# SiLU of two layers' gates: from one ScalarE instruction to a tanh in two halves with the products on GpSimd and VectorE

## The reference

```python
# layer 2
o = jnp.concatenate([oa.reshape(B, S, -1), ob.reshape(B, S, -1)], -1) * jax.nn.silu(gate)
return o @ w_out
...
# layer 3
od = rmsnorm(od, g_sub_d) * (1.0 - lam_init)
o = jnp.concatenate([oc.reshape(B, S, -1), od.reshape(B, S, -1)], -1) * jax.nn.silu(gate)
return o @ w_out
```

## Time and profile before

| | |
|---|---|
| median of 3 runs | 906.92 us (903.67 to 908.23) |
| the profiled execution | 905.25 us, of which its span is 903.4 us |
| busy in the span | TensorE 97%, VectorE 73%, ScalarE 53%, GpSimd 9% |
| instructions | 13206 |

### The profile page before, as it was taken

How to read it: one execution, slowest core, us unless ns; L and a number is a source line. 1 busy time by engine, 2 the same in 40 slices (tenths; PEclk the granted TensorE clock), 3 DMA queues, 4 the chain that set the end, 5 groups by cost and what they waited for, 6 DMA issues and landing times.

```text
span 903.4 us, 13206 instructions
## 1 busy us (share of the span) xinstructions
PE 876.2 (97%) x4896; PEld 719.4 (80%) x4896; DVE 659.9 (73%) x1147; ACT 482.0 (53%) x872; POOL 77.5 (9%) x88
## 2 busy tenths in 40 slices
PE   8999999999999999999999999999889989999998
PEld 7777678888888887777888888888669858878876
DVE  6788876777774468877667777546588767999974
ACT  6367845444454355566544444436456675654771
POOL 2100000000000000000000000001385000122010
PEclk9999999999999999999999999999999999999999
DMA  9673146666666575533666666555954414654311
GB/s 344 225 225 117 45 137 195 186 187 186 188 187 187 159 225 171 158 103 113 204 193 186 187 186 186 186 186 151 237 177 142 133 39 132 198 164 127 87 44 46
DMA packets 96495, 147.58 MB, mean 163 GB/s; under 512 B 6240, under 2 KB 59648, under 8 KB 96304
## 3 DMA queue, kind: packets, MB, share of 16 engines
q1 hardware_dynamic: 94656, 141.63, 50.7%
q0 software_dynamic: 912, 2.41, 1.3%
q10 hardware_dynamic: 864, 2.70, 0.9%
HBM read 145.67 MB, written 1.05 MB: 162 GB/s over the span
## 4 chain that ended last, share of the span: by engine, by line
PE 82%; issue 6%; DVE 5%; DMA 3%; ACT 2%; POOL 1%; SPq 0%; DVEq 0%; ACTq 0%; POOLq 0%
PE ps L2319 17%; PE ps L2203 15%; PE ps L2205 14%; PE ps L2204 14%; PE ps L2321 8%; DMA w_raw<-in_w_in_e 3%; PE ps L2405 3%; PE ps L2382 3%; PE ps L2420 3%; POOL small L777 1%; PE ps L2174 1%; PE ps L2190 1%; DVE w_lo L1352 1%; PE ps L2280 1%; PE ps L2282 1%
## 5 line engine op out<-in xcount | busy, mean ns | idle before, releaser
L1352 DVE TENSOR_TENSOR w_lo<-w_raw,w_hi 128x1024 fp32r<-128x1024 f32 (+1 forms) x261 | 308.4, 1206 | 79.6 <-ACT w_hi L876 77.7
L876 ACT ACTIVATE w_hi<-w_raw 128x1024 fp32r<-128x1024 f32 (+1 forms) x261 | 263.6, 1036 | 111.8 <-DMA w_raw<-in_w_down 44.4
L2319 PE MATMUL ps<-hT,w_hi 128*128 128x512 f32 x640 | 226.5, 399 | 0.0
L2203 PE MATMUL ps<-w_hi,hT 128*128 128x512 f32 (+3 forms) x448 | 174.8, 390 | 7.4 <-ACT z L934 3.8
L2321 PE MATMUL ps<-hT,w_lo 128*128 128x256 f32 x640 | 179.8, 281 | 0.0
L2205 PE MATMUL ps<-w_lo,hT 128*128 128x512 f32 (+3 forms) x448 | 169.6, 379 | 0.0
L2204 PE MATMUL ps<-w_hi,hT 128*128 128x512 f32 (+3 forms) x448 | 169.5, 378 | 0.0
L2319 PEld LDWEIGHTS ps<-hT,w_hi 128*128 128x128 f32 x640 | 120.3, 188 | 29.9
L2321 PEld LDWEIGHTS ps<-hT,w_lo 128*128 128x128 f32 x640 | 120.9, 189 | 0.1
L2203 PEld LDWEIGHTS ps<-w_hi,hT 128*128 128x128 f32 x448 | 84.5, 189 | 29.0 <-issue 10.7
L2205 PEld LDWEIGHTS ps<-w_lo,hT 128*128 128x128 f32 x448 | 84.5, 189 | 15.7
(11 more groups left out here) (264 smaller groups left out, 1180.4 us busy)
## 6 DMA issues: line engine op xcount, KB each, us to landing
w_raw<-in_w_gate_up SPq DMA_DIRECT2D x176, 256.0 KB, 3.2
w_raw<-in_w_down SPq DMA_DIRECT2D x44, 512.0 KB, 3.4
w_raw<-in_w_in_e SPq DMA_DIRECT2D x38, 512.0 KB, 5.5
w_raw<-in_w_qkv_o SPq DMA_DIRECT2D x24, 512.0 KB, 4.0
w_raw<-in_w_in_o SPq DMA_DIRECT2D x20, 512.0 KB, 3.9
w_raw<-in_w_out_e SPq DMA_DIRECT2D x16, 512.0 KB, 3.6
w_raw<-in_w_out_o SPq DMA_DIRECT2D x16, 512.0 KB, 3.7
w_raw<-in_w_in_e SPq DMA_DIRECT2D x8, 268.0 KB, 4.9
```

Of the source, the lines that this page charges most:

```text
L876: n.activation(w_hi[:, u % RING, 0:size], w_raw[:, u % RING, 0:size], ACT.Copy).then_inc(hi_ready, 1)
L1352: v.tensor_tensor(w_lo[:, u % RING, 0:size], w_raw[:, u % RING, 0:size], w_hi[:, u % RING, 0:size].bitcast(F32), ALU.subtract).then_inc(lo ...
L2203: m.matmul(o, lhs[1], rhs[0], start=start, stop=False)
L2319: m.matmul(both, wh[:, k, cols], hT_both[:, :, kk, :], start=kk == 0, stop=False, skip_group_check=True)
```

## The change

In both layers the gates are written as half their value: `rstd_row` is copied with scale 0.5, and layer 3's `gt` steps multiply by 0.5. The step `SILU` goes. In its place stand, on ScalarE, two steps `TH` of 1024 columns each (gates 0 to 3, then 4 to 7), which write tanh of the half gates into another buffer (`hA` in layer 2, `gb` in layer 3). `TH 0` moves ahead, behind `("C", 1, 1)` in layer 3 and `("D", 4)` in layer 2; `TH 1` stands where `SILU` stood. In layer 2 GpSimd makes both products: `GT 0` and `GT 1`, each a multiplication and an addition of 128 x 1024 with a wait between them. In layer 3 GpSimd makes `GT 0`, and VectorE makes the second half in one `scalar_tensor_tensor` of 1024 columns, the step `TG`, between `("SC", 6, 1)` and `("DG",)`. `TH 1` of layer 3 also waits until `GT 0` is done, since it writes the same buffer. `MP` waits for the half that it reads; `ODG` waits for `TG`.

```diff
 ACT_2 = ...
-         ("E", 2, 1), ("C", 1, 0), ("hi", 7, 1), ("hi", 7, 2), ("OS", 0), ("C", 1, 1), ("D", 4), ("E", 3, 0),
-         ("E", 3, 1), ("C", 2, 0), ("hi", 7, 3), ("E", 4, 0), ("E", 4, 1), ("C", 2, 1), ("SILU",),
+         ("E", 2, 1), ("C", 1, 0), ("hi", 7, 1), ("hi", 7, 2), ("OS", 0), ("C", 1, 1), ("D", 4), ("TH", 0), ("E", 3, 0),
+         ("E", 3, 1), ("C", 2, 0), ("hi", 7, 3), ("E", 4, 0), ("E", 4, 1), ("C", 2, 1), ("TH", 1),
 POOL_2 = ...
-          ("WIN", 6), ("POW", "qb"), ("WIN", 7), ("POW", "kb")]
+          ("WIN", 6), ("POW", "qb"), ("WIN", 7), ("POW", "kb"), ("GT", 0),
+          ("GT", 1)]
 ACT_3 = ...
-         ("E", 2, 1), ("D", 4), ("gt", 6, 0), ("hi", 7, 2), ("C", 1, 1), ("E", 3, 0), ("D", 8), ("E", 3, 1),
+         ("E", 2, 1), ("D", 4), ("gt", 6, 0), ("hi", 7, 2), ("C", 1, 1), ("TH", 0), ("E", 3, 0), ("D", 8), ("E", 3, 1),
-         ("hi", 9, 1), ("C", 4, 1), ("OD", 3), ("E", 6, 0), ("gt", 7, 0), ("E", 6, 1), ("SILU",), ("C", 5, 0),
+         ("hi", 9, 1), ("C", 4, 1), ("OD", 3), ("E", 6, 0), ("gt", 7, 0), ("E", 6, 1), ("TH", 1), ("C", 5, 0),
 DVE_3 = ...
-         ("X", 6, 1), ("gt", 7, 1), ("D", 7), ("D", 11), ("SC", 6, 0), ("ODMS",), ("SC", 6, 1), ("DG",), ("X", 7, 0),
+         ("X", 6, 1), ("gt", 7, 1), ("D", 7), ("D", 11), ("SC", 6, 0), ("ODMS",), ("SC", 6, 1), ("TG",), ("DG",), ("X", 7, 0),
-POOL_3 = [("POW", "lora"), ("POW", "qd"), ("POW", "kd"), ("POW", "kc"), ("POW", "qc"), ("ODP",), ("ODG",)]
+POOL_3 = [("POW", "lora"), ("POW", "qd"), ("POW", "kd"), ("POW", "kc"), ("POW", "qc"), ("GT", 0), ("ODP",), ("ODG",)]
...
+    gate_tanh = hA[:, :, :].rearrange("p t (k n) -> p (t k) n", n=T)
...  GpSimd, layer 2
+                pool.wait_ge(sem("gates2_tanh"), at + 1)
+                part, th = gT[:, 4 * at:4 * at + 4, :], gate_tanh[:, 4 * at:4 * at + 4, :]
+                link(g.tensor_tensor(th, th, part, ALU.mult))
+                g.tensor_tensor(part, part, th, ALU.add).then_inc(sem("gates2_ready"), 1)
...  GpSimd, layer 3
+                pool.wait_ge(sem("gates3_tanh"), 1)
+                part, th = gT[:, 0:4, :].rearrange("p k t -> p (k t)"), gb[:, :]
+                link(g.tensor_tensor(th, th, part, ALU.mult))
+                g.tensor_tensor(part, part, th, ALU.add).then_inc(gates_ready, 1)
...
-                pool.wait_ge(gates_ready, 1)
+                pool.wait_ge(sem("gates3_last"), 1)
...  ScalarE, layer 2
-                    n.activation(rstd_row, ps[:, OB + 1, 0:T], ACT.Copy).then_inc(sem("factor_row"), 1)
-                elif what == "SILU":
+                    n.activation(rstd_row, ps[:, OB + 1, 0:T], ACT.Copy, scale=0.5).then_inc(sem("factor_row"), 1)
+                elif what == "TH":
                     for t in range(NT):
-                        act.wait_ge(acc_free[t], DENSE["gate_e"] + 2)
-                    every = gT[:, :, :].rearrange("p k t -> p (k t)")
-                    n.activation(every, every, ACT.Silu).then_inc(sem("gates2_ready"), 1)
+                        act.wait_ge(acc_free[t], DENSE["gate_e"] + at[0] + 1)
+                    g = 4 * at[0]
+                    n.activation(gate_tanh[:, g:g + 4, :], gT[:, g:g + 4, :], ACT.Tanh)\
+                     .then_inc(sem("gates2_tanh"), 1)
...  ScalarE, layer 3
-                                 ps[:, BANK[DENSE["gate_o"]], :], ACT.Copy).then_inc(acc_free[0], 1)
-                elif what == "SILU":
+                                 ps[:, BANK[DENSE["gate_o"]], :], ACT.Copy, scale=0.5).then_inc(acc_free[0], 1)
+                elif what == "TH":
                     for t in range(NT):
-                        act.wait_ge(acc_free[t], DENSE["gate_o"] + 2)
-                    every = gT[:, :, :].rearrange("p k t -> p (k t)")
-                    n.activation(every, every, ACT.Silu).then_inc(gates_ready, 1)
+                        act.wait_ge(acc_free[t], DENSE["gate_o"] + at[0] + 1)
+                    if at[0]:
+                        act.wait_ge(gates_ready, 1)
+                    n.activation(gb.rearrange("p (k n) -> p k n", n=T), gT[:, 4 * at[0]:4 * at[0] + 4, :], ACT.Tanh)\
+                     .then_inc(sem("gates3_tanh"), 1)
...  VectorE, both layers, then layer 3
-            dve.wait_ge(sem("gates2_ready") if stage == "attn2" else gates_ready, 1)
+            if stage == "attn2":
+                dve.wait_ge(sem("gates2_ready"), mix_tile(stage, p) // 4 + 1)
+            else:
+                dve.wait_ge(gates_ready if mix_tile(stage, p) < 4 else sem("gates3_last"), 1)
...
-                    v.tensor_copy(gT[:, 4 * c + 2:4 * c + 4, :].rearrange("p b t -> p (b t)"),
-                                  ps[:, BANK[DENSE["gate_o"]] + 1, :]).then_inc(acc_free[1], 1)
+                    v.tensor_scalar(gT[:, 4 * c + 2:4 * c + 4, :].rearrange("p b t -> p (b t)"),
+                                    ps[:, BANK[DENSE["gate_o"]] + 1, :], 0.5, None, ALU.mult).then_inc(acc_free[1], 1)
+                elif what == "TG":
+                    dve.wait_ge(sem("gates3_tanh"), 2)
+                    half = gT[:, 4:8, :].rearrange("p k t -> p (k t)")
+                    v.scalar_tensor_tensor(out=half, in0=gb[:, :], scalar=1.0, in1=half, op0=ALU.add, op1=ALU.mult)\
+                     .then_inc(sem("gates3_last"), 1)
```

More of the change, by code:

```diff
@@ L840, in _ @@
                 power(at, hrs[:, lo:lo + w], hss[:, lo:lo + w], w)
-            else:
+            elif what == "WIN":
                 if at == 0:
@@ L851, in _ @@
                 power(at[0], hrs[:, lo:lo + 16], hss[:, lo:lo + 16], 16)
+            elif what == "GT":
+                pool.wait_ge(sem("gates3_tanh"), 1)
+                part, th = gT[:, 0:4, :].rearrange("p k t -> p (k t)"), gb[:, :]
+                link(g.tensor_tensor(th, th, part, ALU.mult))
+                g.tensor_tensor(part, part, th, ALU.add).then_inc(gates_ready, 1)
             elif what == "ODP":
```

## The result

The changed kernel takes 914.53 us (median of 4 runs, 914.09 to 915.45) against 907.16 for the kernel before (4 runs): a ratio of 1.0084, 95% interval 1.0057 to 1.0111, or 7.6 us more. Slower was forecast, by 3.0 us.

A forecast was written before the change was run, and what follows sets the result against it. TensorE, busy for 97% of the span, was taken as the bound. Terms +1.1 - 0.4 + 2.3 = +3.0 us on the profiled 905.25 gave 908.25; that execution lay 1.67 below the median, so 909.9 us, range 903.0 to 912.5.

The forecast's parts named there:

- The loads go: ScalarE, layer 2: two table loads and SiLU, 4.47 us, become one tanh of about 1.06 us.
- The lock-out: GpSimd's products, 2.36 us each, shut VectorE out of the shared SBUF port for whole instructions, taking turns.
- all three places named: VectorE: a weight half near 710 over 3 us, a scaling near 721 and a rotation near 841 over 2 us.
- GT 0, layer 2: GpSimd's first-half products delay VectorE's low halves of units (6, 2) and (6, 3): +1.1 us, range 0.2 to 1.6.
- GT 1, layer 2: Second-half products delay X 5 and D 5, leaving 0.15 us at S 6: gain 0.1 to 0.75, taken as 0.4.
- before one of the two the product gets in: Layer 2's GT 1: the product precedes one scaling of SC 4 0, shutting VectorE out until 723.5.
- "no lock-out" rival: GpSimd's products run beside VectorE; S 6 gains 2.1 us, total -3.3, so 903.6 us; chance 0.17.
- the half clock "again": Layer 2, GT 1: TensorE idles from 722.7 to 725.6 in one piece, so the half clock is expected again.
- GT 0, layer 3: Product delays VectorE's last ROT kc, the keys' transposes (1.5 us late), X 3 and T 2 1: +2.3, range 0 to 2.5.
- The tail: Layer 3's end: shorter TH 1 gains nothing, TG fits VectorE's 1.26 us wait; cost nothing, 0.3 if late.
- the clock falls in layer 3 too: Rival: TensorE's idling before the keys' transposes and S 4 brings half clock, price 1.6; sum +5.6, 912.5 us; chance 0.15.
- the forecast's own case: Whole kernel, lock holding: the three terms sum to +3.0 us, giving 909.9 us; chance 0.45.

The follow-up runs named there:

- the cut products: Changed kernel with each of the six GpSimd products cut to a few columns, waits and order kept: 903.58 us, ratio 0.9976 to the kernel before.
- The run with one product: Changed kernel with the multiplication of layer 2's GT 1 left out, so one GpSimd product instead of two: 911.87 us, ratio 1.0060 to the kernel before.
- the kernel with the products on VectorE: Changed kernel with all products on VectorE, one scalar_tensor_tensor per half where VectorE waits, none on GpSimd: 903.04 us, ratio 0.9964 to the kernel before.
- the swap with the products on VectorE: Changed kernel with all products on VectorE and SC 4 0 moved behind X 5 and D 5: 902.84 us, ratio 0.9961 to the kernel before.
- `GT 0` alone: Layer 2 as changed but GT 1 on VectorE, GT 0 on GpSimd; layer 3 as before: 904.80 us, ratio 0.9984 to the kernel before.
- layer 3 alone: Layer 3 as changed, layer 2 with the SiLU of the kernel before: 907.62 us, ratio 1.0021 to the kernel before.
- layer 2 alone: Layer 2 as changed, layer 3 with the SiLU of the kernel before: 910.26 us, ratio 1.0059 to the kernel before.

## Why the prediction was right on the sign and too small in size

*The loads go.* Right: ScalarE has two instructions fewer, no table load between the exponentials, and tanh takes 1.06 us, as worked out.

*The lock-out.* Right, at all three places named, and shown by the cut products (9.8 us less). The Trainium skill's "SBUF — State Buffer" (section "SBUF: two separate sides") says that an exclusive lock is held for a whole instruction; the 2.47 us of a scaling of 0.35 agree.

*GT 0, layer 2: +1.1 forecast, 1.4 measured.* GpSimd won both turns, for which the forecast's bound was 1.6. The order was right instruction by instruction: the low halves were to end at 713.6 and 717.1, and with the 1.1 us by which this execution was late already they end at 714.6 and 717.95. TensorE's two waits there are 0.70 and 0.22 us; half a microsecond more lies beside them, where the rows name no wait.

*GT 1, layer 2: -0.4 forecast, +4.0 measured. This is the step that failed*, in three terms.
The first is the sentence "before one of the two the product gets in". Two products followed each other and two scalings did; the addition went between them. The forecast's own rule, by turns and one whole instruction each, gives just that, and for `GT 0` the forecast had used it; for `GT 1` the addition was given no turn and cost nothing. `X 5` moved not by 2.06 us but by 4.3 (from 3.08 to 7.36 behind `gt 6`). The run with one product shows the size: 2.16 us at `T 3 1`, 1.86 at the output projection, 2.2 in the time.
The second is the way from `T 3 1` to S 6. I let S 6 start 0.8 us behind the start of `T 3 1`; at full clock it is 1.89, because `E 5 1` waits for that transpose. So with one product S 6 comes 1.35 us late, where the sum had it 0.15 early. The same slip made the "no lock-out" rival too good at S 6, 2.1 instead of 0.97. Its total of -3.3 (its own terms, 722.88 + 4.9 against 731.25, give -3.5) was still met by the kernel with the products on VectorE, and so by luck as far as `S 6` goes.
The third is the clock. I had expected the half clock "again", at its old price. But S 6 and `T 4 0` took 2.08 and 1.94 us instead of 1.50 and 1.97, and `T 3 1` 1.09 instead of 0.63.

*GT 0, layer 3: +2.3 forecast, 2.1 by the shift of `T 2 1`, +1.9 by the run alone.* Right. The keys' transposes came 1.25 us late against 1.5 forecast, and the addition cost nothing before `SC 2 0`, since VectorE was reading PSUM meanwhile.

*The tail: nothing forecast.* `TG` ended at 875.76, 0.07 ahead of `ODG`'s start, and the wait of 2.09 us is the old one. What was missed is the clock: I argued from one row that a wait of 2.2 us there passes at full clock. In the changed kernel the same wait was followed by half clock, 1.6 us in its profiled execution. The rival "the clock falls in layer 3 too" had the right price at another place. Whether layer 3's product brings it on stays open: of the profiled executions with that product all four show half clock behind this wait; of the six without it one does (the swap with the products on VectorE), and four have full clock behind waits of 2.08 to 2.19 us. The sixth, `GT 0` alone, has its fall ahead of `OF`:

```profile
864.00:868.00 4.00, 4.00 (x23) 3.59 (x24) 2.51 (x9) 3.59 (x4) 1.98 (x2) 0.81 0.37 127
868.00:872.00 4.00, 3.50 (x18) 2.29 (x17) 4.00 (x9) 2.48 (x3) 2.04 (x1) 0.76 0.01 2
```

TensorE had been busy for 19.98 of the 20 us before 866, so here the clock fell with no wait ahead of it, and no sum of waits of the kind that the rival used foretells it. That fall cost nothing: the wait for `DG` behind it shrank from 2.19 to 0.50 us, and `OF` starts 0.36 us later than in the kernel before, where the first `out` of layer 2 was 0.35 later already. So the product alone isn't what brings the fall, and I have no run that tells what does.

*The range.* Its upper end, 912.5, was a sum with only one shut-out scaling and one more fall of the clock. The second scaling and the longer way to S 6 are missing in every case that holds the lock. As an estimate, with the 2.2 us of the run with one product and the 1.1 of the longer way (1.89 - 0.8), the forecast's own case gives 909.9 + 3.3 = 913.2, above the upper end.

## What to carry to other kernels

Where GpSimd makes large products from SBUF to SBUF, read off which VectorE instructions with operands in SBUF start within them, and count one whole product for each, as many as GpSimd has queued one behind another. VectorE instructions that read PSUM pass; of those in SBUF the reciprocal of four columns did too. A short instruction on the critical path is the worst neighbour: a scaling of 0.35 us became one of 2.47. With the products on the idle engine the change cost 7.6 us, and with the same products on the busy one, 1.22 us each, it gained 3.3.

When one wait is removed, follow the consumer's whole list of conditions to see which is late next. Here the exponential also waited for a transpose to free its buffer, and that took half of the gain expected at `S 6` (0.97 us of 2.1 were left).

## What the runs showed that I had not expected

TensorE's clock goes with much of the spread of one kernel's runs. Over 32 runs of the kernel before, those with a mean granted clock of 0.991 have a mean span of 906.3 us (7 runs), those with 0.992 905.1 (4), those with 0.994 903.3 (12) and those with 0.996 902.7 (9). With the products cut, two runs at 0.998 have spans of 900.1 and two at 0.991 a mean of 905.15. So the mean clock differs from execution to execution with the same program, and the clock of one profile is not the clock of all. Over the 32 runs of the kernel before span times mean clock spreads less than the span (standard deviation 1.2 us against 1.8), though not in every kernel (1.7 against 0.7 with layer 3 alone). Its mean is 898.3 before, 904.6 changed, 901.3 with layer 2 alone, 899.4 with layer 3 alone and 897.0 with the products on VectorE. As an estimate by that measure, 6.3 us of the 8.8 between the mean spans of the changed kernel (4 runs) and of the one before are waits, and the rest, 2.5, is clock; the clock is given to 0.001, which is 0.9 us.

The lock works against GpSimd as well. Its addition beside a weight half lasts 3.27 us (713.60) and 2.34 beside a scaling (726.13); cut to a few columns it lasts 1.06 (709.68) and 0.20 (720.79).
